# Retention scores and values inside the last input chunk: where four groups of small matmuls stand

## The reference

```python
rq_h = apply_rotary(split_heads(rq, N_RET_HEADS), cos, sin)
rk_h = apply_rotary(split_heads(rk, N_RET_HEADS), cos, sin) * (HEAD_DIM ** -0.5)
ret = chunkwise_retention(rq_h, rk_h, split_heads(rv, N_RET_HEADS), log_gamma)
ret = head_group_norm(ret).reshape(ret.shape[0], seq, RET_WIDTH)
ret = (jax.nn.silu(rg.astype(jnp.float32)) * ret).astype(x.dtype)
mixed = jnp.concatenate([fox.astype(x.dtype), ret], axis=-1)
h = h + mixed @ w_out[i]
```

## Time and profile before

| what | value |
|---|---|
| median of 3 runs | 1290.96 us (1290.7 to 1291.1) |
| span of the profiled execution | 1288.7 us |
| median of the runs less the span | 2.3 us |
| TensorE matmul busy | 1276.3 us, 99% |
| VectorE busy | 934.0 us, 72% |
| ScalarE busy | 682.0 us, 53% |
| granted TensorE clock, mean | 0.999 |

### The profile page before, as it was taken

How to read it: one execution, slowest core, us unless ns; L and a number is a source line. 1 busy time by engine, 2 the same in 40 slices (tenths; PEclk the granted TensorE clock), 3 DMA queues, 4 the chain that set the end, 5 groups by cost and what they waited for, 6 DMA issues and landing times.

```text
span 1288.7 us, 20242 instructions
## 1 busy us (share of the span) xinstructions
PE 1276.3 (99%) x7942; PEld 1126.6 (87%) x7942; DVE 934.0 (72%) x1145; ACT 682.0 (53%) x807; POOL 46.5 (4%) x69
## 2 busy tenths in 40 slices
PE   9999999999999999999999999999999999999997
PEld 8988888888998888887888999999988898999996
DVE  5758665566667766558787887777977968877775
ACT  5655444446565444446555654444665556544455
POOL 0000000000132000000100000000200000000000
PEclk9999999999999999999999999999999999999999
DMA  9735555555433655554544455544545535544520
GB/s 379 270 138 219 210 186 190 194 196 188 143 127 132 233 188 184 185 191 168 182 164 147 144 183 196 195 176 183 195 155 188 189 123 189 194 175 186 195 98 33
DMA packets 34542, 232.31 MB, mean 180 GB/s; under 512 B 4016, under 2 KB 4272, under 8 KB 7344
## 3 DMA queue, kind: packets, MB, share of 16 engines
q1 hardware_dynamic: 30960, 218.90, 46.3%
q10 hardware_dynamic: 3520, 12.55, 2.9%
HBM read 228.29 MB, written 1.05 MB: 178 GB/s over the span
## 4 chain that ended last, share of the span: by engine, by line
PE 94%; DVE 4%; ACT 1%; issue 1%; DMA 1%; ACTq 0%; DVEq 0%
PE ring L430 23%; PE ring L426 12%; PE ring L334 7%; PE ring L336 6%; PE ring L335 6%; PE acc L499 5%; PE acc L497 5%; PE acc L498 5%; PE acc L334 5%; PE acc L336 4%; PE acc L335 4%; DVE wlo L326 1%; PE acc L430 1%; PE acc L726 1%; PE ring L497 1%; PE ring L499 1%
## 5 line engine op out<-in xcount | busy, mean ns | idle before, releaser
L326 DVE TENSOR_TENSOR wlo<-raw,whi 128x2048 fp32r<-128x2048 f32 x202 | 462.9, 2297 | 94.8 <-ACT whi L318 94.3
L318 ACT CAST whi<-raw 128x2048 fp32r<-128x2048 f32 x200 | 381.4, 1909 | 87.5 <-PE acc L336 31.0
L430 PE MATMUL ring<-xs,whi 128*128 128x512 f32 x1312 | 328.5, 392 | 0.0
L430 PEld LDWEIGHTS ring<-xs,whi 128*128 128x128 f32 x1312 | 235.9, 189 | 42.2
L426 PEld LDWEIGHTS ring<-xs,wlo 128*128 128x128 f32 x1312 | 176.5, 190 | 13.8 <-issue 1.7
L426 PE MATMUL ring<-xs,wlo 128*128 128x256 f32 x1312 | 185.3, 284 | 0.0
L334 PE MATMUL ring<-xs,whi 128*128 128x256 f32 x512 | 148.0, 289 | 0.1
L335 PE MATMUL ring<-xs,whi 128*128 128x256 f32 x512 | 144.8, 283 | 0.0
L336 PE MATMUL ring<-xs,wlo 128*128 128x256 f32 x512 | 144.8, 283 | 0.0
L334 PE MATMUL acc<-hhi,whi 128*128 128x256 f32 x368 | 104.2, 283 | 0.0
L336 PE MATMUL acc<-hhi,wlo 128*128 128x256 f32 x368 | 104.1, 283 | 0.0
(11 more groups left out here) (373 smaller groups left out, 1850.6 us busy)
## 6 DMA issues: line engine op xcount, KB each, us to landing
raw<-wstream SPq DMA_DIRECT2D x206, 1024.0 KB, 4.8
sq<-lnp ACTq DMA_DIRECT2D x3, 1024.0 KB, 4.7
hT<-xT ACTq DMA_DIRECT2D x4, 256.0 KB, 5.5
raw<-wstream SPq DMA_DIRECT2D x4, 256.0 KB, 5.2
raw<-wstream SPq DMA_DIRECT2D x2, 512.0 KB, 8.6
hT<-xtok ACTq DMA_DIRECT2D x1, 1024.0 KB, 18.8
misc<-decay ACTq DMA_DIRECT2D x1, 1024.0 KB, 4.8
kT<-lnp ACTq DMA_DIRECT2D x1, 1024.0 KB, 4.7
```

What stands on the lines that cost most here:

```text
L318: act.copy(whi[:, c % SPLIT, :], raw[:, c % RAW, :]).then_inc(hi_made, 1)
L326: dve.tensor_tensor(wlo[:, c % SPLIT, :], raw[:, c % RAW, :], whi[:, c % SPLIT, :].bitcast(f32), ALU.subtract).then_inc(lo_made, 1)
L430: mm = pe.matmul(to(b + t), wh[:, w], xs[:, k, :, :].rearrange("p a s -> p (a s)"), start=False, stop=k == NT - 1, skip_group_check=True)
```

## The change

Values 0 and 1 and scores 2 and 3 are no longer issued after chunk 13. `gemm` gets a parameter `late`: with it the callback `between` runs in the second half ahead of tile k = `late`. Chunk 13 is called with `retention` as callback and `late=2`, so the four groups stand after 24 + 6 of its 48 matmuls, in the order values 0, values 1, scores 2, scores 3. After the chunk come values 2 and values 3.

Since bank 1 is then in use by chunk 13, head 7 takes `acc_bank(3)` in place of bank 1. Scores 3 therefore wait for `scaled(12)` (13) in place of `scaled(13)` (14), and for the decays of heads 0 to 3, whose head 3 uses the same bank. Values 1 wait for four decays, as values 0 do; values 2 and 3 wait for all eight. VectorE does `decayed(2)` and `decayed(3)` ahead of `scaled(13)`. This holds for both layers. ScalarE's program and all transfers stay as they are.

```diff
         def ret_bank(h):
 
-            return acc_bank(2 + h % 2) if h // 2 == 1 else bank(h % 2 if h // 2 == 3 else 2 + h % 2)
+            if h // 2 == 3:
+                return acc_bank(3) if h % 2 else bank(0)
+            return acc_bank(2 + h % 2) if h // 2 == 1 else bank(2 + h % 2)
...
                 for t in range(2):
-                    if t and between is not None:
+                    if t and between is not None and late is None:
                         between()
                     for k in range(NT):
+                        if t and k == late and between is not None:
+                            between()
...
                     if i == 3:
-                        pe.wait_ge(gemm_free, FREE[f"in{L}"] + 14)
+                        pe.wait_ge(gemm_free, FREE[f"in{L}"] + 13)
+                        pe.wait_ge(r_m, RET_H * L + 4)
...
                     h = 2 * i
-                    pe.wait_ge(r_m, RET_H * L + (4 if i == 0 else h + 2))
+                    pe.wait_ge(r_m, RET_H * L + (4 if i < 2 else RET_H))
...
+                def retention():
+                    ret_values(0)
+                    ret_values(1)
+                    ret_scores(2)
+                    ret_scores(3)
...
-                        gemm(C_IN[L] + j, in_bank(j))
+                        gemm(C_IN[L] + j, in_bank(j), between=retention if j == 13 else None, late=2)
...
-                ret_values(0)
-                ret_scores(2)
-                ret_values(1)
-                ret_scores(3)
                 ret_values(2)
                 ret_values(3)
...
                         dve.wait_ge(r_rdy, 2 * L + 2)
+                        if j == 13:
+                            decayed(2)
+                            decayed(3)
                         scaled(j, pair(gT, j - 12))
...
-                decayed(2)
-                decayed(3)
                 x_low(X + 1, lambda j: pair(acc, j), [0, 1])
```

More of the change, by code:

```diff
@@ L336, in three, with gemm @@
                 return pe.matmul(o, l2, r1, start=False, stop=stop, **kw)
-            def gemm(c, b, x_need=None, m=0, between=None):
+            def gemm(c, b, x_need=None, m=0, between=None, late=None):
                 pe.wait_ge(lo_made, m * RAW + (c + 1))
```

## The result

The changed kernel takes 1300.26 us (median of 5 runs, 1299.2 to 1300.65) against 1290.81 us. The ratio is 1.0072, with a 95% interval from 1.0061 to 1.0083: it is slower by 9.5 us. I had forecast 1297.0 and a range to 1299.9. The direction was right, and the time lies just above the range. It is between the 1299.3 and the 1301.6 us of the rival in which the clock falls once or twice, which I had given 13% in all.

The account below looks back on a forecast made before the run. TensorE, busy 1276.3 of 1288.7 us, was taken as the bound. Per layer +3.14 less 0.15 = +2.99 us, two layers +6.0; span 1294.7, plus 2.3 to the median, gave 1297.0 us, range 1295.8 to 1299.9.

Parts of the forecast that it names:

- the rival in which the clock falls once or twice: TensorE's clock falls in the idle stretches before the output product: 1299.3 us with one drop, 1301.6 with two; chance 0.13.
- The strand: After chunk 13: ScalarE's weight cast, SiLU, table load, x cast, then VectorE's low half of x, to the product; 5.11 us.
- the product's delay: Output product after chunk 13 starts 2.99 us later per layer: 3.14 us later chunk end less 0.15 us slack.
- The block: Values 0 and 1 and scores 2 and 3 inside chunk 13: 2.95 us on TensorE, 3.31 at old durations.
- The late end of the chunk: Chunk 13 ends 3.14 us later with the four groups inside it, 3.5 us at most.
- The two covers: Decays of heads 0 to 3 finish 0.6 us before values 0 need them; those of heads 4 to 7 before values 2.
- The waiting block: Rival: inside chunk 13, values 0 come before the decays of heads 0 to 3 are done; 1298.8 us, chance 0.05.
- Its own sign of being wrong: In the output product, a granted clock under 1 would point to the rival of a falling clock.
- the step from span to time: The traced span lies 2.3 us under the median of the runs; this distance was kept, from 1294.7 to 1297.0 us.
- The price of a drop: A fall of TensorE's clock after idleness costs about 2.3 us, taken from slow matmuls at the program's start.
- rows 9: Profile rows of 16 equal matmuls at the program's start: 379 ns fastest, 634 median, 794 slowest, over 5.7 us.
- The drain behind the table load: In ScalarE's strand, the skill's 1380 ns drain would add 2.8 us over both layers; the row's 1.29 us was taken.

Follow-up runs that it names:

- the second experiment: The changed kernel with ScalarE casting the first two quarters of x ahead of weight cast, SiLU and table load: 1289.03 us, ratio 0.9987.
- the seventh: The changed kernel with ScalarE casting x after the weight cast but ahead of SiLU and the table load: 1294.39 us, ratio 1.0031.
- the third: The kernel before the change with the two x casts moved ahead of weight cast, SiLU and table load: 1290.63 us, ratio 1.0.
- The filled gap: The changed kernel with eight extra fp32 matmuls behind values 3 in both layers, their result overwritten: 1296.57 us, ratio 1.0048.
- The long gap in the old kernel: The kernel before the change with four idle ScalarE copies ahead of the casts of x: 1303.37 us, ratio 1.0097.
- the short gap in the old kernel: The kernel before the change with two idle ScalarE copies ahead of the casts of x: 1297.16 us, ratio 1.005.
- half of the move: Against the old kernel, only values 0 and 1 inside chunk 13, scores 2 and 3 behind it, VectorE in old order: 1293.87 us, ratio 1.0024.

## Why the prediction missed

**The strand, its place and its length: right.** It was worked out at 5.11 us from L318 to the product and measured 5.19; the product's delay was given as 2.99 us for each layer and measured 3.08 and 3.09 (chunk 13's start to the product's). The block: 2.95 us worked out, from 690.62 to 693.58 2.96 measured. (Of its terms the 0.74 us for values 1 came without a row; 691.32 to 692.07 in the trace after, it is 0.75.) The late end of the chunk, +3.14, was right within 0.05 us (695.93 less 686.84 is 9.09 us, against 5.94 of the old kernel, 693.27 less 687.33: 3.15). The cut strand (the second experiment) and the part of it that was cut (the seventh) show that ScalarE's order sets the product's start in the changed kernel, and the third that in the old one it did not by itself: the decays on VectorE were as late.

**The two covers: right.** Values 0 did not wait for the decays of heads 0 to 3, and values 2 not for those of heads 4 to 7: TensorE's waits in the changed kernel have no entry for either. The waiting block did not come about.

**What follows a gap: the step that failed.** I had the gap right, 3.8 us, twice, and took from it only its own length. The sentence "the idle stretch is bounded by busy ones on both sides" was given as the reason against the clock rival, and the chance for it was 0.13; the range stopped at one drop, although the gap was forecast twice. Its own sign of being wrong, a granted clock under 1 in the product, came about, and with it TensorE's busy time, which was to stay within 1 us, went up by 3.1. The filled gap shows that it is the clock: with the same late start, the 48 matmuls take 5.82 us in place of 7.33 and 8.49. The long gap in the old kernel shows that idleness alone brings it on. The gaps of 3.84 and 4.18 us were followed by a drop in both layers, those of 2.0 and 1.9 us in one of two. So the likeliest case should have had both drops in it, and the sum should have been 1290.96 + 6.2 + 4.1 = 1301.3 us; measured are 1300.26 in the median and 1299.2 in the fastest run. Of the 1.0 us between them, 0.5 is the earlier start of chunk 13 in the first layer, and 0.5 is in the step from span to time: it was taken as 2.3 us, but the run of 1300.26 us has a span of 1298.5, which is only 1.8 us below it.

**The price of a drop: near in size, in part by luck.** From the start of the program I had worked out 2.3 us. Measured were 1.48, 2.64, 2.45, 2.70, 1.45 and 1.46 us, 2.0 in the mean. The matmuls of rows 9 are slow: they take 5.67 us, and sixteen rows of the same size took 3.72 in the filled gap. But the profile gives a granted clock of 1.00 for them (1.25 to 6.92 of the old kernel), so it does not show that the clock is the reason, and the row did not have to carry over. The loss for a matmul is 0.21 less 0.12 us, and what differs is how many of them are slow. The Trainium skill (TensorE: Matmul & The Clock Gate, What's actually happening) says that idleness throttles the array to 1.2 GHz and activity releases it. The traces agree: behind the gap of 2.0 us the granted clock is 0.50 from 1045.40 to 1048.70 and 0.99 from 1048.70 on, and behind the filled gap it is 1.00. I had weighed this too lightly.

**The drain behind the table load: the row was right.** In the changed kernel 698.54 to 699.83 are 1.29 us from the load to the cast behind it, where nothing else is in the way and TensorE waits for it. The 1380 ns of drain that the Trainium skill (ScalarE: Activation LUTs, What ACT_TABLE_LOAD costs) adds does not show.

Open is what decides whether a gap of 2 us brings a drop. The profiles show it in the second layer and not in the first, with the same gap in front.

## What to carry to other kernels

Work that a matmul stream does behind an event is the cover of every strand that starts at this event. Moved ahead of it, it costs the same time on its own engine, and the strand is bare: count the strand through the other engines' orders before moving, and cut it first. And a gap on TensorE of about 2 us or more is to be priced with the slow matmuls that may follow it, here 1.5 to 2.7 us a time, which was 0.4 to 0.8 of the gap.

## What the runs showed of the hardware

TensorE's clock can fall after a gap of only 2.0 or 1.9 us, between matmuls that run at full pace on both sides, and can do so 1 us or more after the gap has ended (the short gap in the old kernel, second layer: 0.12 us a matmul at first, then 0.21 at a granted clock of 0.50). Idle pieces of 1.6 and 0.6 us in the same stretch brought no fall in either layer (half of the move). At the lower level a matmul of 256 columns takes 0.21 us from start to start against 0.12, a factor of 1.8 and not of 2. Eight fp32 matmuls whose result nobody reads (3.72 us of TensorE in each layer) were enough to keep it up and saved 3.7 us over both layers.
